# Two transformer layers on one core: products of constant tiles in TensorE's waits, x scaled before it is turned, keys waited for head by head

## What is computed

```python
h = rms_norm(x, norm1_w)                   # both layers begin so; rows of x are tokens
u = h @ w_in

score = jnp.where(visible, score, -jnp.inf)
_, idx = lax.top_k(score, top_k)           # the indexer's 64 keys
s = jnp.einsum('bqgrd,bqkgd->bqgrk', qg, k_sel) * scale
p = jax.nn.softmax(s, axis=-1)

aff = jax.nn.softmax(jnp.einsum('bld,de->ble', u, w_router), axis=-1)
g, idx = lax.top_k(aff.transpose(0, 2, 1), cap)    # routing: 32 tokens for each expert
xin = jax.vmap(lambda ub, ib: ub[ib])(u, idx)      # gather
hg, hu = xin @ w_gate, xin @ w_up                  # per expert, 1024 x 1024 each
eo = (silu(hg) * hu) @ w_down
```

## Time and profile before

| | us |
|---|---|
| median of 3 runs | 1196.36 (1196.31 to 1196.43) |
| the profiled execution, device time | 1196.45 |
| its span in the trace | 1194.5 |
| TensorE busy | 1098.5 (92%) |
| VectorE busy | 507.0 (42%) |
| ScalarE busy | 419.2 (35%) |
| DMA, mean over the span | 259 GB/s, 309.45 MB |

### The profile page before, as it was taken

One profiled execution on the slowest core, in us unless ns is written; L12 is line 12 of the kernel. 1 busy time (PEld: TensorE's weight loads), 2 busy tenths in 40 slices (PEclk: granted clock), 3 DMA queues, 4 the chain that ended last, 5 costly groups with the idle time before them and its releaser, 6 DMA issues.

```text
span 1194.5 us, 16626 instructions
## 1 busy us (share of the span) xinstructions
PE 1098.5 (92%) x6691; PEld 785.0 (66%) x6691; DVE 507.0 (42%) x999; ACT 419.2 (35%) x800; POOL 16.4 (1%) x28
## 2 busy tenths in 40 slices
PE   7999999999999999999999996998978797879786
PEld 6988988888999999798678885332323232323231
DVE  4778774795666555676875323010101000100011
ACT  4667666844666444664345312000100000000000
POOL 3000000000000000000000000000000000000000
PEclk9999999999999999999999997999999999999998
DMA  8735334343465667254241985799999999999995
GB/s 230 247 116 190 116 130 145 128 157 135 148 211 157 176 163 208 83 199 141 72 141 72 361 333 221 295 427 427 428 427 427 429 427 428 427 428 430 424 422 235
DMA packets 95108, 309.45 MB, mean 259 GB/s; under 512 B 6016, under 2 KB 41096, under 8 KB 83080
## 3 DMA queue, kind: packets, MB, share of 16 engines
q1 hardware_dynamic: 94296, 307.42, 66.8%
q0 software_dynamic: 496, 1.07, 0.4%
q10 hardware_dynamic: 256, 0.10, 0.0%
HBM read 307.53 MB, written 1.05 MB: 258 GB/s over the span
## 4 chain that ended last, share of the span: by engine, by line
PE 72%; DMA 23%; DVE 3%; ACT 1%; issue 1%; SPq 1%; ACTq 0%; DVEq 0%
PE bank L438 71%; DMA parts_room<-in_w_up 7%; DMA arena<-in_w_down 4%; DMA parts_room<-in_w_down 3%; DMA arena<-in_w_up 3%; DMA ring<-in_w_down 3%; DMA xh<-in_w_down 2%; SPq L1137 1%; PE bank L671 0%; DMA arena<-in_x 0%; DVE parts L1689 0%; DVE roots_room L1661 0%; DVE hidden_parts L1901 0%; DVE arena L2218 0%; ACT parts L1262 0%
## 5 line engine op out<-in xcount | busy, mean ns | idle before, releaser
L438 PE MATMUL bank<-parts 128*128 128x256 f32 (+1 forms) x2352 | 299.8, 288 | 1.4 <-issue 1.2
L438 PEld LDWEIGHTS bank<-parts 128*128 128x128 f32 x2352 | 288.3, 191 | 15.2 <-issue 12.0
L1262 ACT ACTIVATE parts<-ring 128x512 fp32r<-128x512 f32 x328 | 203.7, 629 | 227.1 <-PE bank L438 218.2
L1689 DVE TENSOR_TENSOR parts<-ring,parts 128x512 fp32r<-128x512 f32 x328 | 218.9, 689 | 120.5 <-ACT parts L1262 118.7
L438 PE MATMUL bank<-hidden_parts,parts 128*128 128x256 f32 x1024 | 164.9, 283 | 0.0
L438 PE MATMUL bank<-arena 128*32 128x512 f32 (+4 forms) x548 | 149.7, 487 | 11.3 <-DMA arena<-in_w_down 2.7
L438 PE MATMUL bank<-arena,roots_room 128*32 128x512 f32 x400 | 131.6, 607 | 15.4 <-DMA ring<-in_w_gate 5.5
L438 PEld LDWEIGHTS bank<-hidden_parts,parts 128*128 128x128 f32 x1024 | 141.4, 192 | 0.1
L2205 DVE TENSOR_TENSOR sqr<-bank,arena 128x512 f32<-128x512 f32 x8 | 5.2, 686 | 273.5 <-ACT arena L1579 273.5
L438 PEld LDWEIGHTS bank<-arena 128*128 128x128 f32 (+2 forms) x548 | 78.8, 194 | 54.1 <-issue 40.8
L438 PE MATMUL bank<-ring,roots_room 128*32 128x512 f32 x224 | 98.2, 600 | 7.8 <-DMA xh<-in_w_up 4.0
(11 more groups left out here) (300 smaller groups left out, 955.3 us busy)
## 6 DMA issues: line engine op xcount, KB each, us to landing
ring<-in_w_in SPq DMA_DIRECT2D x21, 2048.0 KB, 8.0
arena<-in_w_gate SPq DMA_DIRECT2D x14, 2048.0 KB, 34.6
arena<-in_w_down SPq DMA_DIRECT2D x13, 2048.0 KB, 37.1
arena<-in_w_up SPq DMA_DIRECT2D x11, 2048.0 KB, 36.8
ring<-in_w_ff_in SPq DMA_DIRECT2D x8, 2048.0 KB, 7.8
ring<-in_w_ff_out SPq DMA_DIRECT2D x8, 2048.0 KB, 9.0
parts_room<-in_w_up SPq DMA_DIRECT2D x8, 2048.0 KB, 36.8
ring<-in_w_gate SPq DMA_DIRECT2D x7, 2048.0 KB, 35.3
```

Of the source, the lines that this page charges most:

```text
L438: return nc.tensor.matmul(o, lhsT=l, rhs=r, start=first, stop=last)
L1262: A(w_part[0][:, p % PIECES], piece_of(n, p), ACT.Copy).then_inc(S("pieces rounded"), 1)
L1689: X.tensor_tensor(w_part[1][:, p % PIECES], piece_of(n, p), w_part[0][:, p % PIECES].bitcast(F32), ALU.subtract).then_inc(S("pieces split" ...
```

## The change

- TensorE issues products of constant tiles ahead of its waits (`keep_clock`): 13 of 256 columns of a zeroed tile (set by GpSimd ahead of its own loads) before it waits for the identity; in the routing 7 of 512 columns (identity times the table `iota`) before the wait for the affinities, 11 before that for the ranks, 1 before the picks, 2 after the gather. No one reads their bank.
- The rows of x are scaled themselves, 512 columns at a time, by ScalarE (tile 0) and VectorE (tile 1), and TensorE turns the scaled rows with transposes in place of the products with xdiag. All four banks of x are turned ahead of h.
- `att_scores` waits for the padded keys of its own group; `pad_keys(3)` moves ahead of `round_half(EARLY)` on ScalarE.
- On VectorE `rest_of_half(7)` moves in between the sixth and seventh round of `select_rounds(0, ...)`.
- GpSimd sets `eps` ahead of its loads of vectors.

```diff
--- before.py
+++ after.py
@@ -223,7 +223,7 @@
         xtok = area(0, 2, D)
         vrows = area(2048, 2, P)
         xsquared = area(4128, 2, D)
-        xdiag = area(6176, 2, P)
+        xnormed = area(6176, 2, D)
         rnn = area(0, 8, T + 4)
         decay_a = area(0, 8, T)
         xc = area(2080, 8, T)
@@ -528,6 +528,13 @@
                 mm(ps[:, 0:n], mean_64, sqr[:, i % 2, 0:n]).then_inc(S("head stats"), 1)
 
 
+            def keep_clock(n, b, stationary, moving):
+
+                for _ in range(n):
+                    mm(bank[b][:, 0:moving.shape[1]], stationary, moving)
+
+            pe.wait_ge(S("filler set"), 1)
+            keep_clock(13, 3, sqr[:, 0, 0:P], sqr[:, 0, 0:T])
             pe.wait_ge(S("identity loaded"), 16)
             pe.wait_ge(S("norm loaded"), 16)
             ps = take(0, "norm")
@@ -542,19 +549,17 @@
                         last = nc.tensor.transpose(ps[:, c:c + P], xtok[:, t, k * P:k * P + P], ident)
                 last.then_inc(S("x turned"), 1)
 
-            turn_x(0)
-            turn_x(1)
+            for b in range(4):
+                turn_x(b)
             for b in range(4):
                 ps = take(b, ("h", b))
                 for t in range(TT):
-                    if b == 0:
-                        pe.wait_ge(S(f"x {t} scaled"), 1)
+                    if b % 2 == 0:
+                        pe.wait_ge(S(f"x {t} scaled"), b // 2 + 1)
                     for k in (2 * b, 2 * b + 1):
                         c = (k % 2) * T + t * P
-                        last = mm(ps[:, c:c + P], xtok[:, t, k * P:k * P + P], xdiag[:, t, :])
+                        last = nc.tensor.transpose(ps[:, c:c + P], xnormed[:, t, k * P:k * P + P], ident)
                 last.then_inc(S("h turned"), 1)
-            turn_x(2)
-            turn_x(3)
 
             def turn_vectors(s, n):
                 if s == 0:
@@ -656,7 +661,7 @@
             def att_scores(a):
                 g, q = a // 2, a % 2
                 keys = P * (q + 1)
-                pe.wait_ge(S("keys padded"), 8)
+                pe.wait_ge(S("keys padded"), 2 * g + 2)
                 wait_taken((2 + g // 2, g % 2))
                 for i in range(2):
                     ps = take(4 + i, ("att", a, i))
@@ -950,17 +955,21 @@
                         route_tiles(j - 1)
                 dense_done(last, (n, h))
             route_tiles(3)
+            free_bank = (turn + 1) % 4
+            keep_clock(7, free_bank, ident, C("iota"))
             pe.wait_ge(S("affinity"), 2)
             ps = take(5, "affT")
             for t in range(TT):
                 last = nc.tensor.transpose(ps[0:EXPERTS, t * P:t * P + P], aff[:, t, :], ident)
             last.then_inc(S("affT"), 1)
+            keep_clock(11, free_bank, ident, C("iota"))
             pe.wait_ge(S("ranked"), 1)
             ps = take(6, "slots")
             for t in range(TT):
                 last = nc.tensor.transpose(ps[:, t * EXPERTS:(t + 1) * EXPERTS], rank[0:EXPERTS, t * P:t * P + P],
                                            ident[0:EXPERTS, 0:EXPERTS])
             last.then_inc(S("slots"), 1)
+            keep_clock(1, free_bank, ident, C("iota"))
 
 
             def gather(b, at_g):
@@ -975,6 +984,7 @@
             pe.wait_ge(S("picked"), 2)
             take(6, ("gathered", 6))
             gather(6, slice(0, P))
+            keep_clock(2, free_bank, ident, C("iota"))
             ug = list(use)
             base = seq["dense"]
             at["moe"] = (base, ug)
@@ -1181,9 +1191,10 @@
             act.wait_ge(S("x squares"), 1)
             act.wait_ge(S("x squares by vector"), 1)
             A(xroot, xsq, ACT.Sqrt, scale=1.0 / D, bias=eps).then_inc(S("x root"), 1)
-            act.wait_ge(S("identity loaded"), 16)
             act.wait_ge(S("x scale"), 1)
-            A(xdiag[:, 0, :], ident, ACT.Copy, scale=xscale[:, 0:1]).then_inc(S("x 0 scaled"), 1)
+            for h in range(2):
+                A(xnormed[:, 0, 512 * h:512 * h + 512], xtok[:, 0, 512 * h:512 * h + 512], ACT.Copy, scale=xscale[:, 0:1])\
+                    .then_inc(S("x 0 scaled"), 1)
             wait_taken("norm")
             for b in (0, 2):
                 act.wait_ge(S("h turned"), b + 1)
@@ -1336,8 +1347,8 @@
             round_half(9)
             pad_keys(2)
             half(5, 0)
+            pad_keys(3)
             round_half(EARLY)
-            pad_keys(3)
             half(5, 1)
 
             halves = [(n, h) for n in range(6, 12) for h in range(2)]
@@ -1612,8 +1623,9 @@
             dve.wait_ge(S("x root"), 1)
             X.reciprocal(xscale, xroot).then_inc(S("x scale"), 1)
             dve.wait_ge(S("x scale"), 1)
-            dve.wait_ge(S("identity loaded"), 16)
-            X.tensor_scalar(xdiag[:, 1, :], ident, xscale[:, 1:2], None, ALU.mult).then_inc(S("x 1 scaled"), 1)
+            for h in range(2):
+                X.tensor_scalar(xnormed[:, 1, 512 * h:512 * h + 512], xtok[:, 1, 512 * h:512 * h + 512], xscale[:, 1:2],
+                                None, ALU.mult).then_inc(S("x 1 scaled"), 1)
             for b in (1, 3):
                 dve.wait_ge(S("h turned"), b + 1)
                 for i in range(2):
@@ -1760,9 +1772,10 @@
             index_sum(7)
             filter_argument(2)
             rest_of_half(6)
-            select_rounds(0, range(0, 8))
+            select_rounds(0, range(0, 6))
+            rest_of_half(7)
+            select_rounds(0, range(6, 8))
             key_bias(0)
-            rest_of_half(7)
             wait_taken("q1 stats")
             link(X.reciprocal(q1_scale, q1_root))
             link(X.tensor_scalar(q1_scale, q1_scale, SC1, None, ALU.mult))
@@ -2221,9 +2234,10 @@
         @block.gpsimd
         def _(pool):
             G = nc.gpsimd
+            G.memset(sqr[:, 0, 0:T], 0.0).then_inc(S("filler set"), 1)
+            G.memset(eps, EPS).then_inc(S("constants set"), 1)
             for name, src in vec_loads[1][1::2]:
                 load_rows(pool, name, src, " by pool")
-            G.memset(eps, EPS).then_inc(S("constants set"), 1)
             G.memset(wa, 0.0).then_inc(S("block weights cleared"), 1)
             G.memset(wx, 0.0).then_inc(S("block weights cleared"), 1)
             pool.wait_ge(S("block weights cleared"), 2)
```

## The result

| | us |
|---|---|
| before, median of 16 runs | 1195.89 (1193.30 to 1198.15) |
| after, median of 16 runs | 1198.41 (1195.92 to 1200.58) |
| ratio after to before | 1.0024, 95% interval 1.0016 to 1.0033 |
| the profiled execution of after: device time, span | 1198.76, 1197.0 |

The change makes the kernel slower by 2.9 us (1.9 to 3.9), where 0.45 faster was forecast. The three runs of before that stand ahead of the prediction had spread over 0.12 us; sixteen spread over 4.9.

What follows compares the result with a forecast made beforehand. Bound: the moment transfers resume behind the first expert block (754.55 us), plus a constant, with TensorE's order deciding ahead of it. Begin -0.8, middle -1.95, routing +2.3 sum to -0.45: 1195.9 us, range 1193.8 to 1199.8.

Steps and rivals of the forecast that it cites:

- a clock that rises very late at the begin: At the begin, upper bound: clock rises 8.7 us into the products, fillers end at 11.4, weights' products start 1.5 later.
- Issue to end: From SyncE's first issue behind the expert wait (754.55 before) to the kernel's end: claimed to be a constant.
- Price of a filler: TensorE at full clock: 0.43 us an instruction, 0.86 a 512-column product of two instructions; 256 columns cost half.
- Rival (a): Fillers fit into the waits, a product costing 0.43 us, not 0.86: total -7.65, 1188.7 us; chance 0.09.
- Begin: Start of the kernel: weights' products start at 14.05 instead of 14.87, -0.8 us, bounds -1.6 and +1.5.
- r = 4: At the begin: the clock rises 4 us after the fillers start, so 13 fillers end at 9.1.
- Rival (b): Products of zeros don't raise the clock at the begin: +5.0 there, +5.35 in all, 1201.7 us; chance 0.11.
- The cap that I named: At the begin: ScalarE idles 1.47 us before the square of ik, bounding the gain there to about 1.5.
- Middle: TensorE's waits at 86.67 (0.5 of 0.65 gained) and 105.76 (1.6): -1.95 us, bounds -2.25 and 0.
- Rival (c): The middle's change does nothing, as VectorE sets the pace between 89 and 105: 1197.8 us; chance 0.15.
- Routing: Router's end to first issue behind the expert wait: fillers take about 6.1, give back 2.1 and 1.7; +2.3 us.
- the gather: In the routing: 16 instructions at 0.11 to 0.12 us at full clock, 2.0 instead of 4.07.

Runs made afterwards that it cites:

- six fillers: 6 in place of 13 fillers at the begin, on the changed kernel with 4, 6, 1, 1 fillers in the routing; ratio 0.9972 to the kernel before.
- the two gathers with adjacent columns: Changed kernel with 4, 6, 1, 1 routing fillers, gather reading adjacent columns: ratio 0.9944 with experts' features reordered, 0.9948 with rows written in gather order, both to the kernel before.
- fitting fillers: Changed kernel with 4, 6, 1, 1 fillers in the routing in place of 7, 11, 1, 2; ratio 0.9968 to the kernel before.

## Why the prediction was wrong

The change was forecast to gain 0.45 us and lost 2.9. The measured 1198.41 lies inside the stated range of 1193.8 to 1199.8 only because that range made room for a clock that rises very late at the begin and for a middle that brings nothing. The middle brought all that was forecast, and the late clock cost 0.7 of its 2.3, so that the time lies inside is luck. (The three bounds add up to 1194.4 and 1200.7, not to the 1193.9 and 1200 written there.)

The bound was read right. Issue to end is 440.0 before and 439.7 after, so the moment of the first issue behind the expert wait decided, +2.73 in the traces, and the device times of these two executions differ by 2.31. That this stretch is a constant holds to some 1.6 us only, by the table of marks; in this pair the two happened to agree to 0.3.

*Price of a filler, right.* 14 instructions took 6.26, 22 took 9.61: 0.43 an instruction, 0.86 a product. Rival (a) falls.

*Begin, sign right, size and reason not.* The clock rose later than the r = 4 taken: 13 products ended at 9.8, not 9.1, which with their start at 1.10 instead of 1.35 is r = 6. From there the start of the weights' products came 4.97 later (4.95 forecast), so the trace gave -0.1 where -0.8 was forecast. The runs of this part alone measured -1.7 (-2.7 to -0.6), which may hold the luck in the routing told above. So the sign is right in both, and the size is not settled. Rival (b) falls: the fillers' instructions, all of zeros, stand 0.43 apart up to 7.0 us and 0.22 behind it, so products of zeros did raise the clock. The cap that I named, ScalarE's functions, was the wrong one; transfers of tables and vectors near 19.4 come first, as six fillers showed.

*Middle, sum right, its two terms not.* -1.95 forecast, 695.6 to 693.6 measured. Of the first wait's 0.65 the prediction kept 0.5, and the traces keep 0.15: VectorE reaches the pieces of half 8 at 91.46, as in the kernel before (91.47), so the product that started at 92.48 starts at 92.26, and 0.08 of that is the begin's. The limit was named rightly and its size was not. The second wait brought 1.8 where 1.6 was forecast (105.76 became 103.83, and 0.1 more on the product behind it). That the two errors cancel is luck. Rival (c) falls.

*Routing, the step that failed.* Relative to the router's end:

| step | forecast | traces |
|---|---|---|
| VectorE's first round | +2.1 | +2.2 |
| slots copied | +5.9 | +6.1 |
| gather starts | +5.8 | +6.2 |
| first block starts | +4.0 | +6.4 |
| first issue behind it | +2.3 | +4.8 |

The overruns are as forecast. The step that failed is a term of the sum, the gather: "16 instructions at 0.11 to 0.12, 2.0 instead of 4.07" measured 3.93. I read 0.25 an instruction at half clock and concluded half of that at full clock, without asking what an instruction waits for. The rows of that window could hardly tell, since at half clock adjacent columns take nearly the same (0.21 against 0.23). But the trace of the kernel before had the answer 19 us further on. Its second gather, of the same form, runs at a granted clock of 1.00 (columns as in the earlier trace rows) and takes 4.00:

```profile
755.00:765.00 10.00, 10.00 (x46) 5.35 (x44) 0.00 (x0) 1.14 (x4) 0.00 (x0) 1.00 0.96 387
```
```profile
759.63 4.00 PE L438 MATMUL bank<-arena 128*128 128x128 f32 x16
```

The code says why (`spaced`, every fourth column), and the two gathers with adjacent columns took 1.98 and 1.99. That is 1.9 of the 2.5 missed; 0.4 came with the hand-overs ahead of the gather and 0.1 in the block. With the right gather the sum would have been -0.45 + 1.9 = +1.5: the right sign, and a little short of the measured 1.9 to 3.9; with the begin at the trace's -0.1 it would have been +2.2, within it. (The three parts timed alone also add up to +1.5, but with other terms.)

So the fillers gave back 1.6 in the block, 0.1 in the gather and 0.3 in the turns, and took about 6.8 by running over. The 2.0 given back is what fitting fillers gained.

Of the signs that the prediction named, the 14 instructions, the full clock, the transposes in 1.9 and the missing wait on the padded keys came. The gather of 2.0 did not, nor VectorE's sum near 9.6 (10.28).

## What to carry to other kernels

A filler ahead of a wait must be shorter than the wait that the trace shows, tail and all, else the engine's order turns it into a delay of the same length: 7 and 11 products cost 4.8 us, 4 and 6 gained 2.0. What a full clock gives back is counted instruction by instruction in the stretch, not from the time spent throttled. What an instruction takes at full clock is read from a row of the same form at full clock, if the trace has one, and not halved from one at half clock: the gather took 4.07 at half and 4.00 at full. And a part whose timing hangs on when the clock rises, as the begin here, is not judged by one trace.

## What had not been expected of the hardware

- Loading a 128-column fp32 stationary tile with a stride of four words took 0.24 us at either clock, 16 in 3.81; with adjacent columns 0.12 at full clock, 16 in 1.86.
- Products of zeros alone raised the clock: the first 14 instructions of the fillers stand 0.43 apart, those behind 7.0 us 0.22.
- The clock's rise moves between executions of like kernels: h's 32 instructions took 5.16 in one and 6.26 in another, and sixteen runs of before spread over 4.9 us.
- 32 products took 8.86 us instead of 7.17 after waits of 1.45, 0.46 and 0.78 us within 3.2 us; the granted clock was 0.57 from 22 to 26.
- ScalarE wrote 1024 columns, neighbouring elements 128 columns apart, in 1.8 times the time of adjacent ones (3.92 against 2.18 for two).
